# Strassen-like half products for the r and k tiles of the recurrence, their weight sums on GpSimd and their joins on VectorE

## The chip, the cores and the metric

One core of one Trainium2 chip runs the whole step. The metric is the device time of one execution in microseconds (us). All data are float32.

## The reference, cut to what matters

Two layers of a decoder trunk for 256 prompt positions and 8 single samples, 264 columns in all. Layer 0 is an attention layer with a paged cache, layer 1 an RWKV-7 layer. The changed work is the projection of layer 1 on its r, k and v columns:

```
h = rmsnorm(x, g_pre)                                    # 264 x 2048
p_shift, q_mem, gate = jnp.split(h @ w_in, RWKV_SPLITS, axis=-1)
prev = jnp.concatenate([shift_prev, p_shift[:, :-1]], axis=1)
s = p_shift + (prev - p_shift) * mu
r, k, v, wl, al = jnp.split(s, SHIFT_SPLITS, axis=-1)    # r, k, v: 1536 columns each
...
S = S * w_t + (S @ -kk_t) (kk_t * a_t) + v_t k_t         # per head of 64, over the positions
y_t = S @ r_t
return x + rmsnorm(out @ w_o, g_post)
```

The 24 heads are handled in 12 pairs of heads, 128 columns each of r, k and v.

## The kernel before

The program gives each engine its own list of instructions and orders them by semaphores written out by hand. `hT` holds the normed activations, 16 tiles (k) of 128 rows by T = 264 columns. The weights of a pair (`wrkv`, 128 x 16 x 384, 3 MB) lie in one of two slots `runit`; SyncE (SP) loads the next into the slot that has come free (L635 and L636).

**Turns.** The recurrence is a loop over turns o = -2 to 12 (`turn_of`, one for each engine: TensorE L1140, ScalarE L1636, VectorE L2256). In turn o the weights of pair o + 2 are multiplied ("fill"), pair o + 1 is prepared (token shift, decays, keys, four masked 128 x 512 matrices, the samples' state, the inverses of 16 x 16 blocks), pair o is solved and its outputs formed, and pair o - 1 gets its group norm. Turns 0 to 9 have all of these or all but the last. TensorE's turn is a list of small steps between which twelve calls of `project_part` (L1146) are laid; each does 4 of the 48 matmuls of a pair: parts 0 to 3 are the r tile, 4 to 7 the k tile, 8 to 11 the v tile. A tile accumulates in psum bank 0 or 1 in turn; `p_done` counts finished tiles, `p_free` tiles that were read (it starts at 2).

**ScalarE** copies each tile out in `projected(t)` (L1648): to `pb` (L1663), the last prompt and the sample columns to `shout` (L1664), and scaled by 1 - mu to `pm` (L1665). In the order of its turn: `projected(0)`, the turned rows, the solve's copies, `projected(1)`, more of these, `projected(2)`; then the masked pieces (L1759), two stores (L1763, L1766), and at the start of the next turn a table load and the sigmoids (L1718, L1719). VectorE's `mix` (L2277) waits for all three tiles.

**VectorE** in a turn: mix, keys, the 16-wide diagonal blocks (L2352), decays, normal keys, `scaled` (L2319 to L2322), `level(0)` (L2272), four matrices times masks (L2326), the state (L2401 to L2411), `blocks` (L2333), and the samples' outputs (L2414, L2415), whose end (`prepared`) TensorE's `lora` (L1165) of the next turn awaits. `blocks` is 28 dependent sums and products on 32 partitions (L2341, L2343) that wait for two small DMA steps of SyncE (`blocks` at L603: eight issues at L608, one at L610); in its middle VectorE gives TensorE the scaled state (L2331), for which `from_state` (L1276) waits, ahead of part 9. The solve's end is copied at L2420 to L2426.

**The same trick elsewhere.** The output projections already multiply a 2 x 2 block of weights by a 2 x 2 block of inputs with seven products of half size (`few_products`, L788): 8 matmuls of 132 columns each. There VectorE forms the weight sums (`weight_sums`, L2055 to L2060), the input sums (`input_sums`, L2039 to L2045) and joins the products (`joined`, L2068 to L2077). `w_sum`, `t_sum` and `y_out` count them.

**Around it.** `xT` holds the residual, which is not read between the start of the recurrence and the last residual sum. `qT1` (4 x 264 columns) holds the memory queries of layer 1; after turn -2 only its last 8 columns each are read. GpSimd (POOL) issues the transfers of the attention layer, idles in the recurrence, and issues the last cache loads (L703) when the last pair is solved. After the recurrence SP loads the units of gate and output weights (`late_unit`, L618, DMA at L621).

Of the kernel before, what the change touches and what calls it, by code (L numbers as in the profile page):

```python
# [13 lines left out]
P = 128  # L14
# [6 lines left out]
FH = 12  # L21
# [218 lines left out]
def trunk_step(nc, I, O):  # L240
    ctx = ExitStack()
    with ctx:
# [216 lines left out]

        def few_slot(i):  # L460

            layer, v = FEW[i]
            return (v - PLAIN0) % 3 if layer == 0 else (v + 8) % 3
# [59 lines left out]
        solvedT = nc.dram_tensor("solved_t", (4, 8, BLK * BLK), F32, kind="Internal").ap()  # L523

# [6 lines left out]
        def _(sp):  # L531
# [91 lines left out]
            for o in range(-1, RP - 1):  # L623
# [23 lines left out]
                blocks(o + 1)  # L647
            for v in range(3, 16):
# [47 lines left out]


# [12 lines left out]
        def _(pe):  # L710
# [77 lines left out]
            def few_products(i):  # L788
# [7 lines left out]
                if i >= 2:  # L796
                    pe.wait_ge(sem("y_out"), 2 * (i - 1))
# [12 lines left out]
                pe.wait_ge(sem("t_sum"), 4 * (layer + 1))  # L810
                product(Q4, a22, t4)
                pe.wait_ge(sem("w_sum"), 4 * i + 3)
# [3 lines left out]
                pe.wait_ge(sem("w_sum"), 4 * i + 4)  # L816
# [323 lines left out]
            def turn_of(o):  # L1140
# [5 lines left out]
                def project_part(n):  # L1146
# [6 lines left out]
                    if n == 0:  # L1153
                        pe.wait_ge(sem(f"r_full{b}"), 16 * ((o + 2) // 2 + 1))
                    if n % 4 == 0:
                        pe.wait_ge(sem("p_free"), m + 1)
                    if o == -2 and t == 0:
# [4 lines left out]
                    if n % 4 == 3:  # L1162
                        last.then_inc(sem("p_done"), 1)

# [219 lines left out]
        def _(act):  # L1384
# [15 lines left out]
            def output_tile(layer, j):  # L1400
# [10 lines left out]
                act.wait_ge(sem("y_out"), j - 2 * PLAIN0 + 1 if layer == 0 else 2 * FEW0 + j + 1)  # L1411
# [224 lines left out]
            def turn_of(o):  # L1636
# [11 lines left out]
                def projected(t):  # L1648
# [8 lines left out]
                    m = M_RKV + 3 * (o + 2) + t  # L1657
                    if t == 0:
# [6 lines left out]
                    ac(pm[:, t, :], psum[:, m % 2, 0:T], ACT.Copy, scale=om[:, b, t:t + 1]).then_inc(sem("p_free"), 1)  # L1665

# [127 lines left out]
        def _(dve):  # L1794
# [238 lines left out]
            def input_sums(layer, part):  # L2033
# [3 lines left out]
                done = lambda n: dve.wait_ge(sem("t_sum"), 4 * layer + n)  # L2037
# [9 lines left out]
            def weight_sums(i):  # L2047
# [9 lines left out]
                dve.wait_ge(sem("w_sum"), 4 * i + 1)  # L2057
                tt(s2, s1, a11, ALU.subtract).then_inc(sem("w_sum"), 1)
                dve.wait_ge(sem("w_sum"), 4 * i + 3)
# [196 lines left out]
            def turn_of(o):  # L2256
# [10 lines left out]

                def level(n):
# [129 lines left out]
                if prepare:  # L2398
# [4 lines left out]

# [44 lines left out]
            ch.do(v_.reciprocal(rs1, rs1))  # L2448
# [106 lines left out]
```

## Time and profile before

| | us |
|---|---|
| median of 3 runs (lowest, highest) | 1744.52 (1740.86, 1747.26) |
| the profiled execution: its time | 1743.76 |
| the profiled execution: span of the core | 1742.1 |
| TensorE / VectorE / ScalarE / GpSimd busy | 1622.8 / 1059.1 / 392.3 / 160.8 |
| turns of the recurrence, o = -2 to 12 | about 956 to 1528 |

The span is what the profile's times count from; the profiled execution's own time is 1.7 us longer. A matmul of float32 shows as two MATMUL records and two LDWEIGHTS records (PEld, the weight load beside it). Idle time in brackets is that of the engine just before the instruction, with what ended it. The turns of the recurrence repeat with the same rows; one of them, from TensorE's L1228 at 1250.22 us to its return at 1293.17, is read below.

### The profile page before, as it was taken

To read this page: it belongs to the slowest core of one execution; us is meant where nothing else is said; L and a number is where in the kernel's file an instruction comes from. 1 tells how busy PE (TensorE), PEld (TensorE's weight loads), DVE (VectorE), ACT (ScalarE), POOL (GpSimd) and SP (SyncE) were. 2 spreads that over 40 slices of the span, in tenths; PEclk is the share of its full clock that TensorE was granted. 3 is DMA by queue.
4 is the path that set the end of the run, shared out by engine and by line. 5 is a ranking of instruction groups with operands and counts; after the bars stand their busy time and mean duration, and the time that the engine had idled before them with its cause. 6 is when DMAs were issued, how large, how long until landed. Compare 5 with 4: busy or idle time off the path is not lost.

```text
span 1742.1 us, 27840 instructions
## 1 busy us (share of the span) xinstructions
PE 1622.8 (93%) x9596; PEld 1290.3 (74%) x9596; DVE 1059.1 (61%) x4997; ACT 392.3 (23%) x978; POOL 160.8 (9%) x295
## 2 busy tenths in 40 slices
PE   7979999899999999988989999999999999999995
PEld 6657776677677777657977777777777777788895
DVE  4587555655465555437872467777777777340755
ACT  2112011201121111221120433333333333221011
POOL 1012111221111211220000000000000000020000
PEclk9989999999999999999989999999999999999998
DMA  9579999999999999995442233333332323374441
GB/s 384 206 284 373 420 417 397 379 396 420 405 400 422 418 420 412 357 372 234 146 189 96 102 102 103 101 101 101 101 100 101 102 76 115 108 271 170 145 146 51
DMA packets 101725, 419.95 MB, mean 241 GB/s; under 512 B 41796, under 2 KB 46288, under 8 KB 91984
## 3 DMA queue, kind: packets, MB, share of 16 engines
q0 software_dynamic: 41680, 218.91, 31.6%
q1 hardware_dynamic: 53256, 187.54, 28.4%
q10 hardware_dynamic: 6648, 11.73, 1.8%
q8 instruction: 76, 1.25, 0.3%
q14 instruction: 65, 0.53, 0.1%
HBM read 405.28 MB, written 12.85 MB: 240 GB/s over the span
## 4 chain that ended last, share of the span: by engine, by line
PE 75%; DVE 10%; DMA 6%; ACT 5%; issue 2%; SPq 0%; POOLq 0%; POOL 0%; ACTq 0%; DVEq 0%
PE psum L733 25%; PE psum L801 10%; PE psum L1160 10%; PE psum L783 6%; PE psum L1023 5%; DMA kvr<-in_cv 3%; PE psum L722 2%; PE psum L771 2%; PE psum L1207 2%; DMA kvr<-in_ck 1%; PE psum L1217 1%; PE psum L744 1%; PE psum L759 1%; PE psum L824 1%; ACT gT L1759 1%
## 5 line engine op out<-in xcount | busy, mean ns | idle before, releaser
L1920 DVE CUSTOM_DVE_ANT_0 kvr<-kvr,arena 128x128 f32<-128x128 f32 x1488 | 323.7, 287 | 115.3 <-DMA kvr<-in_ck 115.2
L733 PE MATMUL psum<-hT,wring 128*128 128x264 f32 x1536 | 367.9, 397 | 0.0
L733 PEld LDWEIGHTS psum<-hT,wring 128*128 128x128 f32 x1536 | 294.5, 195 | 67.9 <-issue 19.8
L1160 PE MATMUL psum<-hT,kvr 128*128 128x264 f32 x1152 | 283.3, 392 | 1.8 <-DVE hT L2248 1.8
L1160 PEld LDWEIGHTS psum<-hT,kvr 128*128 128x128 f32 x1152 | 214.0, 192 | 41.9 <-issue 8.9
L1920 DVE DVE_READ_ACCUMULATOR2_ANT arena<- 128x1 f32 x1488 | 122.4, 82 | 0.0
L783 PE MATMUL psum<-hT,kvr 128*128 128x264 f32 x512 | 120.2, 391 | 0.0
L783 PEld LDWEIGHTS psum<-hT,kvr 128*128 128x128 f32 x512 | 96.9, 193 | 16.2 <-issue 0.4
L667 POOL DMA_DIRECT2D kvr<-in_cv x128 | 67.7, 529 | 371.7 <-PE psum L1023 275.0
L1023 PE MATMUL psum<-kvr,arena 128*32 128x384 f32 x1024 | 97.1, 495 | 4.9 <-DMA kvr<-in_cv 4.9
L667 POOL DMA_DIRECT2D kvr<-in_ck x128 | 67.6, 528 | 235.0 <-issue 228.0
L801 PE MATMUL psum<-hT,wring 128*128 128x132 f32 x672 | 77.9, 277 | 0.0
L801 PEld LDWEIGHTS psum<-hT,wring 128*128 128x128 f32 x672 | 76.7, 191 | 0.0
L703 POOL DMA_DIRECT2D wring<-in_cmk x8 | 5.8, 722 | 744.8 <-PE psum L1306 744.8
L1023 PEld LDWEIGHTS psum<-kvr,arena 128*32 128x32 f32 x1024 | 27.0, 109 | 49.8 <-issue 41.2
L733 PE MATMUL psum<-oT,wring 128*128 128x256 f32 x256 | 57.7, 382 | 0.0
L733 PE MATMUL psum<-gT,wring 128*128 128x256 f32 x256 | 57.4, 382 | 0.0
L801 PE MATMUL psum<-gT,kvr 128*128 128x132 f32 x448 | 53.0, 277 | 2.3 <-DVE gT L2030 2.3
L733 PEld LDWEIGHTS psum<-gT,wring 128*128 128x128 f32 x256 | 48.0, 190 | 9.1 <-issue 3.1
L733 PEld LDWEIGHTS psum<-oT,wring 128*128 128x128 f32 x256 | 47.9, 191 | 9.1 <-issue 2.5
L801 PEld LDWEIGHTS psum<-gT,kvr 128*128 128x128 f32 x448 | 51.6, 191 | 3.0 <-DVE gT L2030 1.6
L2326 DVE TENSOR_TENSOR wring<-psum,wring 128x512 f32<-128x512 f32 x48 | 30.9, 686 | 33.2 <-PE psum L1207 32.1
(433 smaller groups left out, 2315.2 us busy)
## 6 DMA issues: line engine op xcount, KB each, us to landing
kvr<-in_ck POOLq DMA_DIRECT2D x128, 768.0 KB, 11.8
kvr<-in_cv POOLq DMA_DIRECT2D x128, 768.0 KB, 11.5
kvr<-in_wrkv SPq DMA_DIRECT2D x12, 3072.0 KB, 13.8
kvr<-in_wo SPq DMA_DIRECT2D x14, 2048.0 KB, 8.1
wring<-in_wkv SPq DMA_DIRECT2D x12, 2048.0 KB, 11.8
wring<-in_wm SPq DMA_DIRECT2D x8, 2048.0 KB, 11.9
wring<-in_wg SPq DMA_DIRECT2D x8, 2048.0 KB, 12.1
kvr<-in_wg SPq DMA_DIRECT2D x8, 2048.0 KB, 9.1
```

The source lines that it names most:

```text
L667: pool.dma_start(ring[:, n % KRING, :], I["c" + name][bass.ds(pid, 1)].rearrange("a p n -> (a p) n"))\
L722: last = mm(psum[:, bank, 0:n], w[:, k, t * P:(t + 1) * P], rhs[:, k, 0:n], start=(k == 0), stop=(k == KT - 1))
L733: last = mm(psum[:, m % 2, 0:n], w[:, k, t * P:(t + 1) * P], rhs[:, k, 0:n], start=(k == 0), stop=(k == KT - 1))
L744: last = mm(psum[:, t, 0:T], w[:, k, t * P:(t + 1) * P], hT[:, k, :], start=(k == 0), stop=(k == KT - 1))
L771: last = mm(psum[:, m % 2, 0:T], w[:, k, t % 2 * P:(t % 2 + 1) * P], hT[:, k, :], start=(k == 0), stop=(k == KT - 1))
L783: last = mm(psum[:, m % 2, 0:T], w[:, k, t * P:(t + 1) * P], hT[:, k, :], start=(k == 0), stop=(k == KT - 1))
L801: last = mm(few_bank(i, q), w[:, k, :], x[:, k, :], start=(k == 0), stop=(k == KT // 2 - 1))
L1023: last = mm(Vp[32 * c:32 * c + 32, 0:384], Ps[:, n % 2, j * FH:j * FH + 32], ring[:, v % VRING, c * 384:(c + 1) * 384], start=(j == 0), st ...
L1160: last = mm(psum[:, m % 2, 0:T], w[:, k, t * P:(t + 1) * P], hT[:, k, :], start=(k == 0), stop=(k == KT - 1))
L1207: last = mm((A, B)[h][:, n * 256:(n + 1) * 256], src[hp, c * P:(c + 1) * P], KR[hp, a, c, :], start=True, stop=True)
L1920: last = v_.tensor_tensor_reduce(page, page, qb[:, n % 2, h * P:(h + 1) * P], 1.0, 0.0, ALU.mult, ALU.add, S[:, n % 2, j * FH + h:j * FH + ...
L2326: tt(GM[:, a, q, :], (A, B)[q % 2], masks[:, K_RM:K_RM + 512], ALU.mult).then_inc(sem("gm_out"), 1)
```

## The change

For pairs 1 to 11 of 0 to 11 (the second to the twelfth) the r and k tiles are taken together as a 2 x 2 block of weights (the halves of k by r and k columns; `pair_weights`), and multiplied by the 2 x 2 block of `hT` (the halves of k by 132 columns) with seven products of eight matmuls. The v tile stays as it was. The rows of the pair, 56 half products and 16 v matmuls (every second of 32 rows), are dealt out to the twelve parts by twelfths. The input sums stand in `xT`, whose contents go to DRAM and back; GpSimd makes them once. GpSimd also makes the four weight sums of each pair: one set of 1024 columns in the memory queries' place (`wsum1`), used twice, and two in place over the weights. Joins are nine operations of VectorE in three groups, and ScalarE copies r and k from `pb` and no longer from psum.

```diff
+        psums = xT[:, :, :].rearrange("p k t -> p (k t)").rearrange("p (s k t) -> p s k t", s=4, k=KT // 2)
+        wsum1 = qT1[:, :, 0:2 * P].rearrange("p h (j n) -> p h j n", j=2)
+        ROWS = [(q, k) for q in (Q2, Q1, Q5, Q4, Q7, Q6, Q3) for k in range(KT // 2)]
+        ROWS += [(Q3 + 1, k // 2) for k in range(2 * KT)]
+        CUT = [len(ROWS) * n // 12 for n in range(13)]
...
             for j in range(2):
                 pair(j, "wrkv", runit[:, j, :], f"r_full{j}")
                 pair(j, "vrkv", vunit[:, j, :], f"v1_full{j}")
+            sp.wait_ge(sem("x_new"), 4)
+            sp.dma_start(xkept, xT[:, :, :].rearrange("p k t -> p (k t)")).then_inc(sem("x_in2"), 16)
             sp.wait_ge(sem("p_done"), M_LORA + 2)
             unit(I["wqm1"], 1, 0)
...
                 blocks(o + 1)
+            sp.wait_ge(sem("p_done"), M_RKV + 3 * RP)
+            sp.dma_start(xT[:, :, :].rearrange("p k t -> p (k t)"), xkept).then_inc(sem("x_in2"), 16)
             for v in range(3, 16):
                 late_unit(v)
...
+            pt_ = nc.gpsimd.tensor_tensor
...
+            pool.wait_ge(sem("at_t"), 2 * MH + FH)
+            for u in range(1, RP):
+                m, at0 = M_RKV + 3 * u, 4 * (FEW0 + u - 1)
+                a11, a12, a21, a22 = pair_weights(u % 2)
+                pool.wait_ge(sem(f"r_full{u % 2}"), 16 * (u // 2 + 1))
+                if u > 1:
+                    pool.wait_ge(sem("w_sum"), at0)
+                    pool.wait_ge(sem("p_done"), m - 1)
+                pt_(wsum1, fold(a21), fold(a22), ALU.add).then_inc(sem("w_sum"), 1)
+                pool.wait_ge(sem("w_sum"), at0 + 1)
+                pt_(a21, a11, a21, ALU.subtract).then_inc(sem("w_sum"), 1)
+                pool.wait_ge(sem("p_done"), m + 1)
+                pt_(wsum1, wsum1, fold(a11), ALU.subtract).then_inc(sem("w_sum"), 1)
+                pool.wait_ge(sem("w_sum"), at0 + 3)
+                pt_(fold(a12), fold(a12), wsum1, ALU.subtract).then_inc(sem("w_sum"), 1)
...
+                def pair_part(n):
...
+                    for at in range(CUT[n], CUT[n + 1]):
+                        q, k = ROWS[at]
+                        if at in (0, 24, 48):
+                            pe.wait_ge(sem("p_free"), m + at // 24 + 1)
+                        if q > Q3:
+                            if at % 2 == 0:
+                                last = mm(psum[:, m % 2, TH:TH + T], w[:, k, 2 * P:3 * P], hT[:, k, :], start=(k == 0), stop=(k == KT - 1))
+                                if k == KT - 1:
+                                    last.then_inc(sem("p_done"), 1)
+                            continue
+                        if k == 0:
+                            if q == Q5:
+                                pe.wait_ge(sem("t_sum"), 8)
+                                pe.wait_ge(sem("w_sum"), sums + 1)
+                            if q == Q7:
+                                pe.wait_ge(sem("w_sum"), sums + 2)
+                            if q == Q6:
+                                pe.wait_ge(sem("w_sum"), sums + 3)
+                            if q == Q3:
+                                pe.wait_ge(sem("w_sum"), sums + 4)
+                        s = wsum1[:, k // 2, k % 2, :]
+                        lhs, rhs = {Q2: (a12, b21), Q1: (a11, b11), Q5: (s, t1), Q4: (a22, t4), Q7: (a21, t3), Q6: (s, t2),
+                                    Q3: (a12, b22)}[q]
+                        last = mm(pair_bank(o, q), s if q in (Q5, Q6) else lhs[:, k, :], rhs[:, k, :],
+                                  start=(k == 0), stop=(k == KT // 2 - 1))
+                        if at in (23, 47):
+                            last.then_inc(sem("p_done"), 1)
...
+                def pair_projected(t):
...
+                    if t == 0:
+                        return
+                    if t == 1:
...
+                        act.wait_ge(sem("y_out"), sums + 1)
+                        ac(pm[:, 1, :], pb[:, 1, 1:T + 1], ACT.Copy, scale=om[:, b, 1:2])
+                        ac(shout[:, 3 * (o + 2) + 1, :], pb[:, 1, NPR:T + 1], ACT.Copy)
+                        ac(pm[:, 0, 0:TH], pb[:, 0, 1:rest], ACT.Copy, scale=om[:, b, 0:1])
+                        return
+                    act.wait_ge(sem("p_done"), m + 3)
+                    act.wait_ge(sem("y_out"), sums + 2)
+                    v = psum[:, m % 2, TH:TH + T]
+                    ac(pb[:, 2, 1:T + 1], v, ACT.Copy)
+                    ac(shout[:, 3 * (o + 2) + 2, :], v[:, NPR - 1:T], ACT.Copy)
+                    ac(pm[:, 2, :], v, ACT.Copy, scale=om[:, b, 2:3])
+                    ac(pm[:, 0, TH:T], pb[:, 0, rest:T + 1], ACT.Copy, scale=om[:, b, 0:1])
+                    ac(shout[:, 3 * (o + 2), :], pb[:, 0, NPR:T + 1], ACT.Copy).then_inc(sem("p_free"), 1)
...
                 solution(0)
-                projected(1)
+                if not -2 < o < RP - 2:
+                    projected(1)
                 right_side(1)
                 right_turned(1)
                 solution(1)
+                if -2 < o < RP - 2:
+                    projected(1)
                 projected(2)
...
+                def joined_pair(part):
...
+                    dve.wait_ge(sem("p_done"), m + part + 1)
+                    if part == 0:
+                        ch.do(v_.tensor_copy(r1_, q(Q1)))
+                        v_.tensor_copy(k1_, q(Q5))
+                        tt(r0_, r1_, q(Q2), ALU.add).then_inc(sem("p_free"), 1)
+                    elif part == 1:
+                        ch.do(tt(r1_, r1_, q(Q6), ALU.add))
+                        ch.do(tt(k0_, r1_, q(Q7), ALU.add))
+                        ch.do(tt(r1_, r1_, k1_, ALU.add))
+                        ch.do(tt(k1_, k1_, k0_, ALU.add))
+                        ch.do(tt(k0_, k0_, q(Q4), ALU.add))
+                        dve.sem_inc(sem("p_free"), 1)
+                        dve.sem_inc(sem("y_out"), 1)
+                    else:
+                        tt(r1_, r1_, q(Q3), ALU.add).then_inc(sem("y_out"), 1)
...
                     ch.do(tt(s3, s3, bs(lw), ALU.mult))
-
+                    joined_pair(0)
                     dve.wait_ge(sem("z_y"), 2 * (o + 1) + 1)
...
                     blocks()
+                    joined_pair(1)
                     dve.wait_ge(sem("z_y"), 2 * (o + 1) + 2)
                     ch.do(tt(x3(Z[:, 1, :]), x3(B), i64, ALU.mult))
                     v_.tensor_reduce(ys[:, a, :], x3(Z[:, 1, :]), AX.X, ALU.add).then_inc(sem("prepared"), 1)
+                    joined_pair(2)
...
+            dve.wait_ge(sem("x_in2"), 48)
             for c in range(4):
                 residual(c, rs1).then_inc(sem("x_out"), 1)
```

`joined_pair` and `pair_projected` do their work in turns -1 to 9. Three products of a pair share a psum bank (`pair_bank`): Q2, Q1, Q5 in the first, Q4, Q7, Q6 in the second, Q3 and the v tile in the first again. The input sums of GpSimd are four 128 x 1056 operations behind a wait for the copy of `xT` out and for `hT`.

## Rows read from the trace of the kernel before

**Rows 1.** One turn by windows: PE, PEld, DVE, ACT, POOL busy; PEclk, DMA, GB/s.

```profile
1079.30:1121.92 42.62, 41.00 (x234) 32.05 (x234) 33.16 (x86) 15.06 (x42) 0.00 (x0) 1.00 0.32 103
```

**Rows 2.** Chain of waits, one turn: start, us, what.

```profile
1254.72 1.78 PE psum L1160 x8
...
1257.72 1.28 DVE wring L2326 x2
...
1269.81 0.36 DVE arena L2331
...
1276.85 0.05 ACT arena L1663
...
1281.59 0.37 DVE arena L2293
```

**Rows 3.** Chain of waits: half products of layer 0; turn -1.

```profile
879.93 17.56 PE psum L801 x156
...
1001.75 3.78 PE psum L1160 x8
```

**Rows 4.** VectorE's groups by form, 780 to 900 us: busy us, mean ns.

```profile
L2055 DVE TENSOR_TENSOR wring<-kvr 128x1024 f32<-128x1024 f32 x6 | 7.3, 1219 | 0.0
...
L2072 DVE TENSOR_TENSOR arena<-arena,psum 128x132 f32<-128x132 f32 x6 | 1.8, 294 | 8.3 <-PE psum L801 8.3
```

**Rows 5.** Timeline of VectorE and TensorE, one turn.

```profile
1261.22 0.69 DVE L2405 TENSOR_TENSOR gT<-psum,arena 128x512 f32<-128x512 f32 x1 [1.03 <-PE psum L1217]
...
1266.69 0.16 DVE L2341 TENSOR_TENSOR kmT<-kmT 32x14 f32<-32x14 f32 x1 [1.87 <-DMA kmT<-near]
...
1274.74 0.69 DVE L2415 TENSOR_REDUCE arena<-gT 128x8 f32<-128x512 f32 x1
...
1277.86 0.29 DVE L2420 COPY gT<-psum 128x128 f32<-128x128 f32 x1 [2.44 <-PE psum L1306]
...
1289.96 1.95 PE L1160 MATMUL psum<-hT,kvr 128*128 128x264 f32 x8
...
1290.56 0.43 DVE L2319 TENSOR_TENSOR wring<-arena 128x256 f32<-128x256 f32 x1 [0.26 <-ACT arena L1734]
```

**Rows 6.** Timeline of ScalarE, 1277 us.

```profile
1277.14 0.17 ACT L1664 ACTIVATE arena<-psum 128x9 f32<-128x9 f32 x1
1277.20 0.48 ACT L1665 ACTIVATE arena<-psum,arena 128x264 f32<-128x264 f32 x1
1277.56 0.51 ACT L1759 ACTIVATE gT<-wring 16x64 f32<-16x64 f32 x2
```

**Rows 7.** Timeline of TensorE, turns -1 and 0.

```profile
998.01 1.08 PE L1193 MATMUL psum<-cst,arena 128*128 128x128 f32 x6 [2.25 <-DVE arena L2322]
...
1024.14 0.68 PE L1171 MATMUL psum<-arena,kvr 96*128 96x264 f32 x2 [2.31 <-DVE arena L2415]
```

**Rows 8.** L1920 on VectorE: durations in ns, smallest, median, largest.

```profile
L1920 DVE CUSTOM_DVE_ANT_0 kvr<-kvr,arena x1488: 272/288/298, 62.9 to 711.4; 128x128 f32<-128x128 f32 x186
```

**Rows 9.** Windows of 910 to 925 us, columns as in rows 1.

```profile
910.00:915.00 5.00, 5.00 (x17) 3.40 (x16) 4.90 (x6) 3.54 (x9) 0.00 (x0) 0.68 1.00 423
...
920.00:925.00 5.00, 5.00 (x25) 3.64 (x24) 0.00 (x0) 0.00 (x0) 0.00 (x0) 1.00 0.01 2
```

**Rows 10.** Timeline of SyncE's issues, and of TensorE at 1528 us.

```profile
925.60 0.33 SPq L546 DMA_DIRECT2D wring<-in_wqm  x1
...
1491.06 62.25 SPq L621 DMA_DIRECT2D kvr<-in_wg  x4
...
1528.33 1.97 PE L783 MATMUL psum<-hT,kvr 128*128 128x264 f32 x4
```

**Rows 11.** DMA issues: count, KB each, us from issue to landing.

```profile
xT<-in_xT SPq DMA_DIRECT2D x1, 2112.0 KB, 8.0
```

**Rows 12.** TensorE by windows, turn -1: PE busy, PEclk, DMA, GB/s.

```profile
1000.00:1005.00 5.00, 5.00 (x16) 0.50 0.15 41
...
1025.00:1030.00 5.00, 5.00 (x27) 1.00 0.67 180
```

More of the change, by code:

```diff
@@ L694, in _ @@
                     page("v", *((kring, "k_full") if in_keys else (vring, "v_full")), n, STREAMS[i], n - KST[i])
+            pt_ = nc.gpsimd.tensor_tensor
+            pool.wait_ge(sem("x_in2"), 32)
+            pool.wait_ge(sem("h_out"), 16)
+            lo, hi = hT[:, 0:KT // 2, :], hT[:, KT // 2:KT, :]
+            b11, b12, b21, b22 = lo[:, :, 0:TH], lo[:, :, TH:T], hi[:, :, 0:TH], hi[:, :, TH:T]
+            t1, t2, t3, t4 = (psums[:, n, :, :] for n in range(4))
+            pt_(t1, b12, b11, ALU.subtract).then_inc(sem("t_sum"), 1)
+            pt_(t3, b22, b12, ALU.subtract).then_inc(sem("t_sum"), 1)
+            pool.wait_ge(sem("t_sum"), 4 + 1)
+            pt_(t2, b22, t1, ALU.subtract).then_inc(sem("t_sum"), 1)
+            pool.wait_ge(sem("t_sum"), 4 + 3)
+            pt_(t4, b21, t2, ALU.subtract).then_inc(sem("t_sum"), 1)
+            pool.wait_ge(sem("at_t"), 2 * MH + FH)
[13 more added lines that the diff above has]
+                pt_(fold(a12), fold(a12), wsum1, ALU.subtract).then_inc(sem("w_sum"), 1)
             pool.wait_ge(sem("y_y"), 2 * RP)
@@ L796, in few_products @@
                 if i >= 2:
-                    pe.wait_ge(sem("y_out"), 2 * (i - 1))
+                    pe.wait_ge(sem("y_out"), 2 * (i - 1) + 2 * UNITS1 * layer)
                 def product(q, w, x):
@@ L815, in few_products @@
                 product(Q7, s3, t3).then_inc(sem("few_y"), 1)
-                pe.wait_ge(sem("w_sum"), 4 * i + 4)
+                pe.wait_ge(sem("w_sum"), 4 * (i + UNITS1 * layer) + 4)
                 product(Q3, s4, b22).then_inc(sem("p_done"), 2)
@@ L1163, in project_part @@
                         last.then_inc(sem("p_done"), 1)
+                def pair_part(n):
+                    a11, a12, a21, a22 = pair_weights(b)
+                    t1, t2, t3, t4 = (psums[:, i, :, :] for i in range(4))
+                    b11, b21, b22 = hT[:, 0:KT // 2, 0:TH], hT[:, KT // 2:KT, 0:TH], hT[:, KT // 2:KT, TH:T]
+                    sums = 4 * (FEW0 + o + 1)
+                    m = M_RKV + 3 * (o + 2)
+                    for at in range(CUT[n], CUT[n + 1]):
[25 more added lines that the diff above has]
+                            last.then_inc(sem("p_done"), 1)
                 def lora():
@@ L2266, in turn_of @@
                 zt = x3(Z[:, 0, :])
+                def joined_pair(part):
+                    if not -2 < o < RP - 2:
+                        return
+                    m, lhs, rest = M_RKV + 3 * (o + 2), slice(1, 1 + TH), slice(1 + TH, 1 + T)
+                    r0_, r1_, k0_, k1_ = pb[:, 0, lhs], pb[:, 0, rest], pb[:, 1, lhs], pb[:, 1, rest]
+                    q = lambda n: pair_bank(o, n)
+                    dve.wait_ge(sem("p_done"), m + part + 1)
[13 more added lines that the diff above has]
+                        tt(r1_, r1_, q(Q3), ALU.add).then_inc(sem("y_out"), 1)
                 def level(n):
```

36 lines of the change are left out of this document (29 added, 7 removed).

## Prediction, made before the changed kernel ran

> **What bounds the kernel now.** The stage that changes, the recurrence, is a steady machine: nine of its turns take 42.6 to 43.0 us each, of which TensorE is busy 41.0 us, VectorE 33.2 and ScalarE 15.1, with a granted clock of 1.00; GpSimd does nothing there [rows 1]. TensorE busy for 41.0 of 42.6 us invites the reading that every matmul removed is time won. The chain of waits says otherwise [rows 2]. Read one turn from 1250.2 us on: TensorE holds the chain until 1257.7 us, then VectorE masks two matrices (L2326), SyncE issues eight small transfers, two transfers follow, VectorE solves blocks from 1266.7 us, and its L2331 at 1269.8 us releases TensorE's L1276. Only then does the chain run over projection parts 9, 10 and 11, to 1276.8 us. There it leaves TensorE again: ScalarE copies the v tile out (L1663 to L1665), copies six masked pieces, loads a table and computes the sigmoids for which VectorE's L2293 waits; the two hand on to each other until VectorE releases TensorE's L1228, where the next turn begins. So of twelve parts of the projection the chain holds four (4, 9, 10, 11); the others are filler beside VectorE, ScalarE and transfers.
>
> **What the half products give.** For pairs two to twelve, 32 matmuls of 264 columns become 56 of 132. A matmul is two records; the eight records of a part, four matmuls of 264, take 1.78 us in the chain, 0.445 us a matmul [rows 2]. 156 records of L801, the same half product elsewhere, take 17.56 us, 0.225 us a matmul [rows 3]. So 14.24 us become 12.60: 1.64 us less TensorE work a pair, 18 us over eleven. On the chain it is less. The 88 rows of the new list are dealt out by twelfths: part 4 holds seven half products (1.58 us for 1.78: 0.20 us less), parts 9 and 11 still four v matmuls, part 10 three (1.34 for 1.78: 0.44 less). That is all the chain can gain, 0.64 us a turn, and the 0.44 counts only if TensorE's last matmul still releases ScalarE.
>
> **The joins on VectorE.** Each is 128x132 with an input in PSUM: 0.29 us as at L2072 [rows 4], about 0.31 with the wait for its own semaphore. The first group (two copies, one sum, 0.9 us) stands between L2402 and L2405, where VectorE idles 1.03 us: nothing. Were that idle time gone, the 1.87 us before L2341, spent waiting for a transfer, would still cover it [rows 5]. The second group, five chained sums, 1.55 us, stands between the blocks and L2414; the third, one sum, 0.31 us, behind L2415. Before, VectorE finished L2415 at 1275.43 us and then idled 2.44 us [rows 5]; now the last join is through at 1275.43 - 0.20 + 1.55 + 0.31 = 1277.09 us. ScalarE began on the v tile at 1276.85 us and now waits for that join (the new wait on y_out; queued behind it are the masked pieces, the table and the sigmoids, and VectorE waits for those). That is 0.25 us later, and it takes the place of TensorE's gain. Behind the wait ScalarE has five operations for three: one more copy of 132 columns, one of nine. By the steps from start to start, 0.06 us after L1664 and 0.36 after L1665 [rows 6], half of the latter plus the former, 0.24 us, is the lower bound and 1.5 times the latter the upper, 0.54; I take 0.40, nearer the middle since a copy of half the columns costs over half. So the tail of a turn costs 0.65 us, ten times (turns 0 to 9): 6.5 us. In turn -1 TensorE waits for L2415 itself, 2.31 us already [rows 7], and the five sums less the 0.20 add 1.35 us. Together about 8 us. The r and k copies that leave the middle of ScalarE's turn save nothing: it idles there.
>
> **The weight sums on GpSimd.** Four a pair, 128x1024. No row has GpSimd arithmetic. The nearest is VectorE's own sum of that shape, 1.22 us (L2055) [rows 4]; I take d = 1.22 us as the lower end, twice that, 2.44, as the upper (an engine fetching its two inputs in turn), and the middle, 1.83. They are in time in any case: the third and fourth have from row 23 (part 3) to rows 40 and 48 (parts 5 and 6), over 10 us; the first two need the next unit, which lands 13.8 us after its issue, a turn ahead. Behind them GpSimd's queue has only cache loads after the last turn. The question is what they do to VectorE, which reads the same SBUF. GpSimd issuing transfers leaves VectorE's two-input L1920 alone, 272 to 298 ns over 1488 [rows 8]; nothing shows GpSimd reading operands. The price lies between nothing (independence) and one engine standing while the other runs. No row is nearer to either; I take the second at somewhat better than even, since both would read two full-rate operands from the same partitions, a load that no row shows borne without loss.
>
> Then place decides. The first two sums are released by row 47 in part 6, about 1265.2 us: they end at 1265.2 + d and 1265.2 + 2d. VectorE's blocks, 28 chained sums of 0.2 us with gaps into which GpSimd can slip, want to start at 1266.5 us and lose (1.83 - 1.3) + 1.83 = 2.4 us. The third sum is released by row 23, the second row of part 3, which began at 1289.96 us; that is some 0.1 us before VectorE's L2319 to L2322, four operations with both inputs in SBUF and on the chain, which stand idle 0.26 us before [rows 5]: 1.7 us. The fourth falls beside L2272 and the reciprocal, with one SBUF operand each. Sum: 3d - 1.4 = 4.1 us a turn, 45 us over eleven.
>
> The Trainium skill (SBUF — State Buffer, Who interferes with whom) has it that a VectorE instruction with two SBUF inputs and a GpSimd instruction that reads SBUF exclude each other for the whole instruction; no run shown here can confirm it. The same skill's GPSIMD Engine Reference (Elementwise — side-by-side cycle accounting) gives GpSimd's sum 1.96 times VectorE's; by it the collisions would be 5.8 us a turn and the time near 1816.
>
> **The residual and the queues.** The copy of xT out, 2112 KB, enters SP's queue about 911 us; the transfers of that moment run at 423 GB/s and are through before 920, when the DMA engines stand idle to 925 [rows 9]; the next issue, L546, comes at 925.60 [rows 10]. 2112 KB at that rate are 5.0 us: it fits. Without the gap the memory queries would wait those 5 us once. The copy back stands ahead of L621 at 1491.06 us; it and the unit's load, 8.0 us each as the residual's load before [rows 11], end before 1528.33, when TensorE first turns to that unit [rows 10]. The four input sums on GpSimd run beside turn -2 and are wanted some 20 us later. All nothing.
>
> **Sum.** 8 + 45 = 53 us on the profiled execution's 1743.76 us (span 1742.1; the median of the runs, 1744.52, is 0.8 us more): 1797 us. With d from 1.22 to 2.44 the collisions are 2.3 to 5.9 us a turn, and the time 1777 to 1817.
>
> **Rivals.** *A: no collision.* Only the joins and ScalarE's two operations are left: 1752 us; ScalarE's bounds make it 1750 to 1753, and a step of 0.08 us either way in each of the six joins on the path 1745 to 1758. For it: no row shows a conflict. Against: none of them could. *B: faster.* TensorE's own queue, not the chain, sets the turn, and the 1.64 us come off each: 1726 us. It decides at L1663, where ScalarE would have to go on earlier than 1276.85 us. For it: 41.0 of 42.6 us busy [rows 1]. Against: VectorE's idle 2.44 us were the only room in the tail, and 1.86 us of joins go into it. *C: collisions, and the clock.* TensorE would stand some 2.4 us before L1276 and 1.7 before L1193. In turn -1 it stood 2.25 us before L1193, the granted clock was then 0.50 for 5 us (1.2 for 2.4 GHz), and eight records took 3.78 us for 1.78; after the 2.31 us at 1024 the clock stayed at 1.00 [rows 3, 7, 12]. One such loss of 2.0 us a turn is 22 us more, 1819; two are 1841.
>
> **How the numbers follow.** Forecast 0.50, A 0.25, B 0.12, C 0.13. A measurement of this kernel tells about 0.5% (8.7 us) from no change. Faster: nearly all of B, 0.11. Within: A up to 1753, 0.15, and edges, 0.17. Slower: the rest, 0.72. The range leaves out B and the worst of C: 1746 to 1834.
>
> **What would show it.** Turns of 46 to 48 us for 42.6; L2319 to L2322 or the blocks' sums with durations or gaps of a microsecond and more where a GpSimd sum runs; ScalarE's copy of v released by the last join; TensorE waiting for L2331. Turns of 43.3 us with VectorE's durations unchanged would be A; under 42 us, B; v matmuls at half speed, C. GpSimd sums above 3 us, or TensorE waiting on w_sum, would break the sum in another place.

## The result: 1808.0 us, 3.7% slower, and the profile after

The changed kernel takes 1808.01 us, the median of 4 runs (1803.30 to 1809.51), against 1742.69 for the kernel before beside it: a ratio of 1.0374, 95% interval 1.0351 to 1.0396. The forecast was 1797 with a range of 1746 to 1834. The profiled execution took 1808.59 us, its span is 1806.9 and its mean granted clock 0.958 (0.980 before).

The page's first part, of the changed kernel: busy time, share of the span, instructions of each engine.

```profile
span 1806.9 us, 29104 instructions
PE 1644.6 (91%) x10124; PEld 1325.5 (73%) x10124; DVE 1150.5 (64%) x5096; ACT 389.7 (22%) x967; POOL 281.5 (16%) x343
```

For this stage the page misleads twice. TensorE, from which 18 us of work were taken, was busy 1622.8 us before and is now at 1644.6. VectorE, which got some 2.5 us of joins a pair (28 us over eleven), has risen by 91 us, from 1059.1. Both engines are busy with the same work for longer. The windows say where: turn -1, turn 1, a steady turn and the last with half products (columns as in rows 1).

```profile
989.04:1033.91 44.87, 33.43 (x179) 26.94 (x178) 34.00 (x77) 9.14 (x20) 10.11 (x4) 0.81 0.24 80
1080.92:1133.04 52.12, 43.03 (x284) 35.19 (x283) 44.11 (x94) 14.85 (x41) 10.26 (x4) 0.93 0.25 84
1237.47:1285.25 47.78, 43.02 (x283) 35.46 (x283) 41.39 (x95) 14.85 (x39) 10.07 (x4) 0.93 0.32 109
1467.55:1510.86 43.31, 41.11 (x284) 34.38 (x283) 37.22 (x94) 14.83 (x39) 4.72 (x2) 0.96 0.24 75
```

A steady turn takes 47.78 us (turns 2 to 8, seven of them, 47.77 to 47.80) where it took 42.62 [rows 1]. TensorE is busy 2.0 us longer than before although it has 1.64 us less to do: the granted clock is 0.93 for 1.00. The last turn has two GpSimd sums for four and 43.31 us; that alone points at the sums.

The chain of waits of the steady turn, of the changed kernel (start, us, what). Its lines for those of rows 2 and 5: L2514 is the third group norm's product, L2557 the last product over the samples' state (it stands right before the blocks), L2487 the blocks, L2477 was L2331, L1370 was L1276, L1237 the v tile's matmuls, L2412 the last join, L1783 and L1784 are ScalarE's copies behind it.

```profile
1245.01 1.73 DVE arena L2513
1246.77 2.27 DVE gT L2514
...
1259.52 2.73 DVE gT L2557
1262.24 2.25 DVE kmT L2487
...
1267.43 0.36 DVE arena L2477
1267.84 1.22 PE psum L1370 x2
1269.06 2.84 PE psum L1237 x8
...
1273.73 1.85 PE psum L1237 x8
1275.60 0.30 DVE arena L2412
...
1276.45 0.37 ACT arena L1783
1276.82 0.29 ACT arena L1784
```

The order is that of rows 2, but without SyncE and its transfers: VectorE, held up, reaches the blocks after their transfer has landed. The new link, join to ScalarE, is there; in this turn the last join itself idles 0.69 us until TensorE's v tile (L1237) is through, so the five joins before it are covered. Three VectorE instructions have grown: 2.27, 2.73 and 2.25 us, 7.25 together. The timeline of GpSimd and VectorE in the same turn shows beside what.

```profile
1243.93 2.37 POOL L750 TENSOR_TENSOR arena<-arena,kvr 128x1024 f32<-128x1024 f32 x1 [27.27 <-PE psum L1254]
1246.38 2.35 POOL L752 TENSOR_TENSOR kvr<-kvr,arena 128x1024 f32<-128x1024 f32 x1
1259.03 2.67 POOL L746 TENSOR_TENSOR arena<-kvr 128x1024 f32<-128x1024 f32 x1 [10.30 <-PE psum L1254]
1261.78 2.68 POOL L748 TENSOR_TENSOR kvr<-kvr 128x1024 f32<-128x1024 f32 x1
```

```profile
1243.47 0.42 DVE L2468 TENSOR_TENSOR arena<-arena,gT 128x256 f32<-128x256 f32 x1
1243.80 1.21 DVE L2418 TENSOR_TENSOR gT<-vmr,psum 128x1024 f32<-128x1024 f32 x1
1244.93 1.80 DVE L2513 RECIPROCAL arena<-arena 128x264 f32<-128x264 f32 x1
1246.77 2.25 DVE L2514 SCALAR_TENSOR_TENSOR gT<-gT,lnv,arena 128x264 f32<-128x264 f32 x1
...
1258.79 0.69 DVE L2555 TENSOR_TENSOR arena<-arena,gT 128x512 f32<-128x512 f32 x1
1259.52 2.73 DVE L2557 TENSOR_TENSOR gT<-arena 128x512 f32<-128x512 f32 x1
1262.17 2.31 DVE L2487 TENSOR_TENSOR kmT<-kmT 32x14 f32<-32x14 f32 x1
```

Read the ends. L746 ends at 1261.70; L2557, 0.69 us elsewhere, ends at 1262.25. L748 ends at 1264.46; L2487, 0.16 us for 32x14 elements, ends at 1264.48. A VectorE instruction that meets a GpSimd sum stands until the sum is over, whatever its own size, and a sum that comes while a VectorE instruction is under way stands too: L746 and L748 take 2.67 for 2.36 us. But L2418, with one of its inputs in psum, and the reciprocal, with one input, run beside L750 at 1.21 and 1.80 us, as ever.

TensorE behind this, of the changed kernel:

```profile
1263.33 1.94 PE L1237 MATMUL psum<-hT,kvr 128*128 128x264 f32 x8
1267.84 1.22 PE L1370 MATMUL psum<-wring,arena 128*128 128x256 f32 x2 [2.57 <-DVE arena L2477]
1268.85 3.04 PE L1237 MATMUL psum<-hT,kvr 128*128 128x264 f32 x8
```

It stands 2.57 us until L2477 is through, and the next eight records take 3.04 us where those before took 1.94: that is the granted clock, 0.50 (1.2 of 2.4 GHz) from 1267.84 to 1269.00 us, and 1.00 again from 1271.90 on.

### The profile page after: what moved, and what is told of

It reads as the page before. It is cut to its first block, busy times and chain, and to the rows that moved or that the text cites. A ratio compares the mean times of both kernels' runs of the same rounds, so it can differ in the third digit from the quotient of the medians.

```text
span 1806.9 us, 29104 instructions
## 1 busy us (share of the span) xinstructions
PE 1644.6 (91%) x10124; PEld 1325.5 (73%) x10124; DVE 1150.5 (64%) x5096; ACT 389.7 (22%) x967; POOL 281.5 (16%) x343
## 4 chain that ended last, share of the span: by engine, by line
PE 69%; DVE 18%; ACT 6%; DMA 5%; issue 2%; SPq 0%; POOLq 0%; ACTq 0%; POOL 0%; DVEq 0%
PE psum L789 25%; PE psum L857 10%; PE psum L839 6%; PE psum L1079 5%; PE psum L1237 3%; PE psum L778 2%; DVE kmT L2487 2%; PE psum L827 2%; DMA kvr<-in_cv 2%; PE psum L1254 1%; DMA kvr<-in_ck 1%; DVE gT L2557 1%; PE psum L1322 1%; PE psum L1301 1%; DVE gT L2514 1%
## 5 line engine op out<-in xcount | busy, mean ns | idle before, releaser
L789 PE MATMUL psum<-hT,wring 128*128 128x264 f32 x1536 | 362.5, 392 | 0.0
L789 PEld LDWEIGHTS psum<-hT,wring 128*128 128x128 f32 x1536 | 289.9, 192 | 66.6 <-issue 19.7
L839 PE MATMUL psum<-hT,kvr 128*128 128x264 f32 x512 | 121.7, 394 | 0.0
L839 PEld LDWEIGHTS psum<-hT,kvr 128*128 128x128 f32 x512 | 97.5, 194 | 16.9 <-issue 0.4
L1237 PE MATMUL psum<-hT,kvr 128*128 128x264 f32 x352 | 99.0, 428 | 0.0
L1237 PEld LDWEIGHTS psum<-hT,kvr 128*128 128x128 f32 x352 | 73.9, 217 | 20.0 <-issue 6.0
L857 PEld LDWEIGHTS psum<-hT,wring 128*128 128x128 f32 x672 | 76.7, 190 | 0.0
L1254 PE MATMUL psum<-hT,kvr 128*128 128x132 f32 x528 | 72.7, 287 | 0.0
L1254 PEld LDWEIGHTS psum<-hT,kvr 128*128 128x128 f32 x528 | 69.2, 200 | 1.4
L750 POOL TENSOR_TENSOR arena<-arena,kvr 128x1024 f32<-128x1024 f32 x11 | 26.2, 2380 | 279.6 <-PE psum L1254 279.6
L789 PEld LDWEIGHTS psum<-oT,wring 128*128 128x128 f32 x256 | 47.8, 190 | 10.4 <-issue 2.5
```

The source lines that it names most:

```text
L750: pt_(wsum1, wsum1, fold(a11), ALU.subtract).then_inc(sem("w_sum"), 1)
L789: last = mm(psum[:, m % 2, 0:n], w[:, k, t * P:(t + 1) * P], rhs[:, k, 0:n], start=(k == 0), stop=(k == KT - 1))
L839: last = mm(psum[:, m % 2, 0:T], w[:, k, t * P:(t + 1) * P], hT[:, k, :], start=(k == 0), stop=(k == KT - 1))
L857: last = mm(few_bank(i, q), w[:, k, :], x[:, k, :], start=(k == 0), stop=(k == KT // 2 - 1))
L1237: last = mm(psum[:, m % 2, TH:TH + T], w[:, k, 2 * P:3 * P], hT[:, k, :], start=(k == 0), stop=(k == KT - 1))
L1254: last = mm(pair_bank(o, q), s if q in (Q5, Q6) else lhs[:, k, :], rhs[:, k, :], start=(k == 0), stop=(k == KT // 2 - 1))
```

## The experiments

The time is told apart in steps, from the whole change down, then built up again in a better order. All times are medians of at least 4 runs; the kernel before took 1741.9 to 1743.0 us beside them.

**1. Without any GpSimd sum.**

```
-pt_(wsum1, fold(a21), fold(a22), ALU.add).then_inc(sem("w_sum"), 1)
+pool.sem_inc(sem("w_sum"), 1)
```

and so for all four weight sums and the four input sums.

> The changed kernel with the four input sums and the forty-four weight sums on GpSimd left out (GpSimd only counts its semaphores on; the half products are made with whatever stands in their place), all joins, waits and matmuls kept. Theory (a GpSimd instruction that reads SBUF and a VectorE instruction that needs two SBUF reads exclude each other for their whole length): VectorE's L2557, L2487 and L2514 go back to 0.69, 0.16 and 0.49 us, a turn takes 43.0 to 43.5 us instead of 47.8, turn -2 is 4 us shorter, and the time is 1748 to 1757 us. Rival (the loss is in the joins, ScalarE's tail and the new waits, and VectorE's long records are waits that would be there anyway): above 1780 us.

1757.63 us (1756.13 to 1758.89), ratio 1.0082 [1.0061, 1.0104]. The sums cost 50 us. The time is 0.6 us above the range of the theory, less than its runs scatter. What is left, 15 us over the kernel before, is twice the 8 of the prediction, and the turns differ among themselves: 42.76 us at a clock of 1.00, up to 45.05 at less. Windows of this kernel: three of 5 us in the longest turn, the shortest turn, and the longest.

```profile
1197.12:1202.12 5.00, 4.73 (x34) 4.34 (x34) 3.58 (x14) 4.10 (x13) 0.00 (x0) 1.00 0.40 106
1202.12:1207.12 5.00, 2.29 (x6) 1.36 (x7) 4.05 (x9) 2.42 (x4) 0.00 (x0) 0.79 0.93 347
1207.12:1212.12 5.00, 5.00 (x25) 4.90 (x25) 4.33 (x10) 3.27 (x7) 0.00 (x0) 0.53 0.88 335
1242.17:1284.93 42.76, 39.79 (x284) 32.77 (x283) 35.62 (x94) 14.58 (x39) 0.00 (x0) 1.00 0.31 103
1197.12:1242.17 45.05, 42.07 (x283) 35.35 (x283) 35.80 (x95) 15.21 (x40) 0.00 (x0) 0.92 0.29 98
```

Early in a turn TensorE has parts 0 and 1 beside a chain of small operations between VectorE and ScalarE. Seven half products last 1.74 us where eight records of 264 columns lasted 1.94, and TensorE is busy only 2.29 of 5 us. Where that is followed by a clock of 0.53, the turn is long.

**2 and 3. GpSimd writes only; GpSimd copies.** The weight sums become `nc.gpsimd.memset(wsum1, 0.0)` (and so on), or `nc.gpsimd.tensor_copy(wsum1, fold(a21))` and so on.

> The changed kernel without the input sums, and with each weight sum replaced by a GpSimd memset of the same place and shape (128 x 1024), behind the same waits: GpSimd writes SBUF but reads nothing. Theory (what collides is GpSimd's reading): VectorE's instructions keep their lengths and the time is that of the kernel without sums, 1748 to 1757 us. Rival (any GpSimd instruction with an SBUF operand holds VectorE up): VectorE has records of over 1.5 us beside every memset, and the time lies above 1765 us.

> The changed kernel without the input sums, and with each weight sum replaced by a GpSimd copy of the same output and of one of its inputs: GpSimd reads one operand instead of two. Theory: a reader of one operand excludes VectorE's two-input instructions just the same, for as long as the copy takes; with copies of 1 to 1.5 us the time is 1760 to 1780 us, and VectorE's first two-input instruction beside a copy is longer by up to the copy. Rival (only an engine reading two streams takes VectorE's share away): as without sums, 1748 to 1757 us.

1757.82 us (1753.94 to 1762.04) with the writes, the same as with nothing there; 1763.0 (1759.75 to 1771.07) with the copies. L2557 in one line each (the durations are smallest, median and largest, ns): the changed kernel, writes, copies.

```profile
L2557 DVE TENSOR_TENSOR gT<-arena x12: 691/2726/2740, 1022.8 to 1543.2; 128x512 f32<-128x512 f32 x12
```

```profile
L2557 DVE TENSOR_TENSOR gT<-arena x12: 691/693/694, 1010.2 to 1488.7; 128x512 f32<-128x512 f32 x12
```

```profile
L2557 DVE TENSOR_TENSOR gT<-arena x12: 691/1405/1406, 1010.5 to 1498.9; 128x512 f32<-128x512 f32 x12
```

It is GpSimd's reading that holds VectorE up, not its writing, and not its being at work. A copy, at 1.04 to 1.38 us, does it too, for as long as it lasts.

**4. The kernel before, with 44 idle sums.** GpSimd adds the same weights into an unused tile, released as in the change; nothing reads the results, and the next load of a unit waits for them.

```
+pt_(scratch4, a21, a22, ALU.add).then_inc(sem("aside"), 1)
```

> The kernel before, nothing of the change in it but forty-four GpSimd sums of two 128 x 1024 blocks of the pair's weights into a place that nobody reads, released by the tiles nearest to where the change releases them (the k tile of the pair before, the r tile of the pair). All outputs are as before. Theory: the collisions alone are the larger part of the loss; GpSimd's sums take 2.4 to 2.7 us, a turn takes 46 to 48 us, and the time is 1782 to 1805 us. Rival (the loss needs the joins and half products, because TensorE's cover has become thinner): below 1755 us.

1801.49 us (1798.21 to 1808.74), ratio 1.0351 [1.0318, 1.0383]. Without half products, joins, new waits of TensorE on the sums or a moved residual, 59 us are lost. In this kernel the sums held VectorE in other places (in a turn 2.21 us in the group norm's product for 0.49, and 2.25 and 2.39 us in two of the blocks' sums for 0.19 and 0.20), and a turn took 47.8 us as well. Nothing of the loss needs the change's own structure.

**5. The changed kernel without the input sums.**

> The changed kernel with GpSimd's four sums over the inputs left out (their results are wrong, the semaphores are kept); the 44 weight sums stay. Theory (collisions, turn by turn): the turn before the first pair shrinks from 34.1 us to the kernel before's 30.1, the rest stays: 1804 us. Rival (the input sums cost nothing, as the prediction had it): 1808 us and that turn at 34.1.

1800.69 us (1796.74 to 1804.70), 7.3 us less by the medians, with some 4 us of scatter on either. The trace shows the 4.0 us that the theory named: from its first half part to the next turn's start, turn -2 takes 30.10 us for 34.11 (957.68 to 987.78; 954.93 to 989.04). The turns from -1 to 9 take 522.4 us for 521.8, so the rest of the 7.3 is not the recurrence's. The timelines of VectorE and TensorE in turn -2 of the changed kernel show how: two 128x256 TENSOR_SCALAR, 0.62 us without sums, meet input sums.

```profile
960.24 3.19 DVE L1949 TENSOR_SCALAR gT<-gT,arena 128x256 f32<-128x256 f32 x2
...
963.48 0.80 PE L892 MATMUL psum<-cst,gT 128*128 128x128 f32 x4 [2.11 <-DVE gT L1949]
```

**6. The sums where VectorE reads psum or waits.** Nothing left out; GpSimd gets further waits, as

```
+pool.wait_ge(sem("tl_in"), u)
 pt_(wsum1, wsum1, fold(a11), ALU.subtract).then_inc(sem("w_sum"), 1)
```

> The changed kernel with nothing left out; GpSimd additionally waits, so that its sums run beside VectorE work that does not read two inputs from SBUF: input sums each behind a head of the memory's weights, sum 1 behind the first joins of r and k of the pair before, sum 2 behind the cumulated decays (beside the reciprocal), sum 3 behind the four scaled tiles, sum 4 behind the first masked product. Theory (the loss of the sums is exclusion with VectorE's instructions of two SBUF inputs, a matter of the moment): turns of 43 to 45 us as without sums, 1757 to 1766 us. Rival 1 (GpSimd's sums slow VectorE or TensorE whatever runs beside them): above 1785. Rival 2 (TensorE now waits for sums that come too late): turns above 46 with idle time of TensorE ahead of half products released by GpSimd.

1763.68 us (1760.17 to 1765.58), ratio 1.0116 [1.0090, 1.0143]. The same 48 sums on the same engine, 44 us less. One was still ill placed (timelines of GpSimd and VectorE of this kernel, lines 9 lower than in the changed one):

```profile
1296.86 2.35 POOL L755 TENSOR_TENSOR kvr<-kvr 128x1024 f32<-128x1024 f32 x1 [9.42 <-DVE arena L2461]
```

```profile
1296.97 2.40 DVE L2465 TENSOR_SCALAR arena<-arena 128x264 f32<-128x264 f32 x1
1299.40 1.80 DVE L2466 RECIPROCAL arena<-arena 128x264 f32<-128x264 f32 x1
```

The wait for sum 2 was meant for the reciprocal, 0.4 us later. The TENSOR_SCALAR ahead of it has one input, and stands for the whole sum all the same, 2.40 for 0.29 us.

**7. No sums, and another deal of the rows.** To the first experiment:

```
-CUT = [len(ROWS) * n // 12 for n in range(13)]
+CUT = [0, 7, 21, 28, 34, 41, 48, 54, 62, 68, 74, 82, 88]
```

> The changed kernel without any GpSimd sum (semaphores only; wrong results, as in the first experiment, which took 1757.6), and with the 88 rows dealt otherwise over the 12 parts: the second part, which covers TensorE's waits for the key sums early in a turn, holds 14 rows for 7, the later ones 6 or 7 for 7 or 8. Theory (part of the 15 us that are left without the sums is TensorE's clock, which falls after waits that the thinner half products no longer cover): the mean granted clock rises from 0.968 towards 0.99, turns fall from 43.9 to about 42.7, 1742 to 1748 us. Rival (the joins and ScalarE's two further copies on the path at a turn's end make up those 15 us): no change, 1755 to 1760.

1748.87 us (1743.99 to 1752.31), ratio 1.0033 [1.0017, 1.0050]: 8.8 us less than with the even deal, for the same instructions. Turns are 42.3 to 42.4 us, some 43.3 to 43.6. The mean clock of the whole execution went from 0.968 to 0.977, not to the 0.99 expected (the kernel before has 0.98). In the turns themselves the theory holds: with the even deal the granted clock was 1.00 in two of the turns 1 to 9 and 0.92 to 0.96 in seven, with this deal 1.00 in all nine. The four turns of 43.3 to 43.6 us are long for another reason: in them VectorE waits 1.7 to 2.0 us ahead of the blocks for SyncE's small transfers, in the five others 0.7 to 0.8.

**8. Placed sums and that deal.**

> Both together, nothing left out: the sums placed as in the second kernel, the rows dealt as in the third. Theory: 1742 to 1752 us, so level with the kernel before. Rival (the first half product that needs a sum now comes right after the turn's start and waits for GpSimd's first sum, and the clock falls again): 1760 to 1775.

1774.71 us (1772.38 to 1778.63), ratio 1.0176 [1.0153, 1.0199]: the rival's figure, but not by the rival's way. Sum 2 again stretched the TENSOR_SCALAR (L2465, median 2398 ns), and with fewer half products beside it TensorE stood longer behind it, 2.5 us in nearly every turn, for 0.5 to 2.4 with the even deal. Its timeline in this kernel, where the eight L1331 take 1.16 us at the full clock:

```profile
1269.49 1.14 PE L1296 MATMUL psum<-cst,arena 128*128 128x128 f32 x6 [2.49 <-DVE arena L2477]
1270.62 2.08 PE L1331 MATMUL psum<-gT 128*128 128x128 f32 x8
```

**9 and 10. The placement mended, with the even deal and with the other.** Sum 2 now waits for the four scaled tiles, sum 3 for the first masked product, sum 4 for the second level's difference; for the second of the two also

```
+CUT = [0, 7, 21, 26, 32, 40, 48, 54, 62, 68, 74, 82, 88]
```

> The placed sums moved once more, nothing left out. In the trace of the first placement (1763.7 us) sum 2 stretched the scaled keys' lower bound, a TENSOR_SCALAR of one SBUF input, from 0.29 to 2.40 us on the chain. Now sum 2 waits for the four scaled tiles, sum 3 for the first masked product, sum 4 for the second level's difference; sum 1 stays behind the first joins. Theory: turns of 45.2 us lose about 1.5 to 2.1 us, 1744 to 1757 us, at or below the 1757.6 without sums. Rival (TensorE's waits at the turn's end set the turn, the stretched instruction was covered): 1760 to 1765.

> As the second placement, with the rows dealt so that the second part holds 14 of the 88 rows and the two parts behind it 5 and 6. Theory (thin cover early in the turn costs clock and time, as 1748.9 against 1757.6 us without sums showed): 1744 to 1752 us, 5 to 10 us under its sibling with the even deal. Rival (the first placement's 1774.7 with this deal against 1763.7 without it: fewer half products around the four scaled tiles let the clock fall there, whatever the sums do): 1765 to 1775.

1751.39 us (1746.75 to 1762.18), ratio 1.0074 [1.0044, 1.0105], and 1747.16 (1744.91 to 1754.13), ratio 1.0030 [1.0012, 1.0048]. The TENSOR_SCALAR is back at 0.29 us. Of the sums' 50 us nothing measurable is left; the 6 us by which the first lies under the kernel without sums is within the scatter of its five runs, and the deal's gain is smaller than without sums (the intervals touch).

**11. The second group of joins ahead of the blocks.**

```
-blocks()
 joined_pair(1)
+blocks()
```

> As the kernel with placed sums and the other deal, and the five joins of the second group ahead of the blocks' small inverses instead of behind them, where VectorE waits 0.76 us for the diagonal blocks' transfer anyway; sum 1 waits for the end of the blocks. Theory (the joins behind the blocks lie on the chain that ends a turn): 0.5 to 0.8 us less a turn, 1736 to 1744 us. Rival (the blocks start 0.85 us later, the state's scaling with them, and TensorE waits for it): no gain, or up to 6 us more.

1745.64 us (1743.09 to 1747.27), ratio 1.0019 [1.0008, 1.0030]. The gain, 1.5 us, is under what was expected and within the scatter of the runs: the profile gives 42.56 us a turn at a clock of 1.00, and shows TensorE waiting 0.76 us for the state's scaling, which stands inside the blocks and now comes later. So part of the rival holds. The best form of the change, then, is level with the kernel before (0.1 to 0.3% over it) and not faster. A window of one of its turns:

```profile
1192.31:1234.88 42.57, 39.77 (x285) 32.78 (x283) 35.55 (x94) 14.74 (x41) 9.44 (x4) 1.00 0.31 103
```

GpSimd is as busy as in the changed kernel (9.44 for 10.07 us a turn), and VectorE at 35.55 for 41.39: the 5.8 us between are standing, not work.

**12. Neither sums nor joins.** To the first experiment; the nine joins are left out, their semaphores kept, the even deal.

> The changed kernel without any GpSimd sum (as the first experiment, 1757.6 us) and also without VectorE's nine joins of r and k (their semaphores are kept, r and k keep old values); the half products, the even deal of the rows and ScalarE's eight copies stay. What is left against the kernel before is the half products with ScalarE's two further copies. Theory (the prediction's sum: the joins cost 8 us, the half products save 7): 1749 to 1751 us here is a confirmed join price, but the half products then save nothing and cost 7 to 8 us through their thin cover. Rival 1 (the joins are all of what is left): 1740 to 1744. Rival 2 (the joins lie beside TensorE's work and cost nothing): 1755 to 1759.

1740.91 us (1737.99 to 1742.33, 12 runs), ratio 0.9985 [0.9975, 0.9995]: rival 1. A turn of this kernel at the full clock:

```profile
1234.23:1276.17 41.94, 39.53 (x285) 32.70 (x283) 33.13 (x85) 14.73 (x40) 0.00 (x0) 1.00 0.31 105
```

## Why the prediction was right, and where it was off

By medians the change now comes apart so: kernel before 1742.7; half products and ScalarE's two copies -2 (1740.9); joins +17 (1757.6); weight sums where the change lets them run +43 (1800.7); input sums +7 (1808.0), of which the trace shows 4. In the profiled executions the turns -1 to 9 took 461.7, 460.4, 473.6, 522.4 and 521.8 us in this order, so joins 13 and weight sums 49. The shares also depend on the order of leaving out: put on the kernel before, the weight sums cost 59.

**The half products: too small on the chain.** The step said that of 1.64 us of TensorE's work only 0.64 a turn come off; less ScalarE's two further copies, priced at 0.40, that is 0.24 without sums and joins. At the full clock a turn went from 42.62 to 41.94 us, 0.68. The chains of a turn of 42.63 us of the kernel before, and of the turn of 41.94 us:

```profile
1121.92 1.16 PE psum L1228 x8
...
1134.01 1.98 PE psum L1160 x8
...
1146.36 1.85 PE psum L1160 x8
...
1148.69 0.37 ACT arena L1665
1149.06 0.12 ACT gT L1759
```

```profile
1250.09 1.16 PE psum L1322 x8
...
1273.48 1.85 PE psum L1237 x8
...
1275.93 0.37 ACT arena L1783
1276.30 0.29 ACT arena L1784
...
1276.69 0.12 ACT gT L1882
```

From the turn's L1228 (L1322) to the end of the last v matmul TensorE takes 25.24 us for 26.29, so the half products give 1.05 us, not 0.64. From ScalarE's scaled copy of v to its masked pieces it is 0.76 us for 0.37: the two copies cost 0.39, as priced (0.40). The step that was off is the reading of the chain. Of the turns 1 to 9 of the kernel before, the one of rows 2 is the only one whose chain runs through SyncE and its transfers; it took 42.96 us. In the other eight TensorE holds the chain from its L1228 through parts 4 to 11, eight parts and not four.

Over eleven turns 0.68 would be 7 us, and 2 were measured (1740.91 to the 1743.04 beside it): other turns of that kernel took 42.3 to 43.7 us. In five of its turns 1 to 9 VectorE waits 1.7 to 2.4 us ahead of the blocks for SyncE's small transfers (42.4 to 43.7 us a turn), in the four others 0.5 to 1.1 (41.9 to 42.3); in those five, and only there, the chain runs through these transfers. The same waits of 1.83 and 1.87 us in two turns of the kernel before lengthened these by only 0.3 to 0.4 us. Only two of the five long turns have a lower clock (0.96). So the thinner cover gave the rest back in two ways, to transfers that it no longer hides and to the clock, and the first took at least as much; why the transfers take longer in some turns, no run here shows.

**The joins: right at the full clock, the total not.** The step let the joins swallow TensorE's 0.64 us and add 0.25, together 0.89 a turn; at the full clock a turn went from 41.94 to 42.76 (42.51 in the kernel of experiment 2), 0.6 to 0.8 us, and in that turn ScalarE does wait for the last join. Half products, joins and ScalarE's copies together were priced at 0.65 us a turn and are only 0.1 at the full clock (42.76 to 42.63), since the half products gave more. Yet they cost 15.5 us in all and not 8. What was left out is what waits do beyond their length. In experiment 1 the granted clock was under 1.00 in seven of the turns 1 to 9, and in four VectorE waited 1.9 to 2.3 us for the small transfers; dealt otherwise, the same instructions took 8.8 us less, with the clock at 1.00 in all nine. Rival C had TensorE's clock after a wait, but only behind collisions.

**The collisions: mechanism right, two places wrong, and the size a little low.** 45 us were priced, 43 measured for the weight sums (49 by the traces of the recurrence). The parts differ more. d was 2.36 us, and 2.67 where a VectorE instruction was already under way, not 1.83; the upper bound, 2.44, would have been nearly right. The first two sums met VectorE where the step said, at the end of part 6, but one instruction earlier: L2557 stood 2.03 us extra, L2487 2.15; less the idle time before the blocks that this used up. The third was released right behind the four scaled tiles in place of 0.1 us before them: those ran undisturbed. TensorE's clock had moved it: in the steady turn L1322, ahead of row 23, took 1.92 us at the half clock, in turn 1, at the full clock, 1.05. The fourth, free by the step, outlasted the reciprocal and stretched L2514 by 1.76. What a microsecond decides shows in turn 1 of the changed kernel, where the third sum came 0.1 us after the first scaled tile and not 1.5:

```profile
1094.79 2.57 DVE L2466 TENSOR_TENSOR wring<-arena,gT 128x256 f32<-128x256 f32 x1
1097.28 2.56 DVE L2467 TENSOR_TENSOR arena<-arena,gT 128x256 f32<-128x256 f32 x1
```

Two instructions of 0.42 us, and a turn of 52.12. The steady turns grew by 47.78 - 42.62 = 5.2 us, of which half products, copies and joins are 0.1 at the full clock; the rest, 5.1, stands against the 4.1 of the sum, and some 1.6 of it is TensorE's clock behind L1370, which the sum left to rival C. That 45 and 43 lie so close is in part luck: with the measured 2.36 in the step's own places the sum is 3 x 2.36 - 1.4 = 5.7 us a turn, 62 over eleven; the third sum mostly missed, the fourth hit unforeseen, and the kernel without the sums was already 7 us slower than the step had it.

**The rule of the Trainium skill.** The page SBUF — State Buffer, Who interferes with whom, which no run could confirm before, fits: a VectorE instruction with two SBUF inputs and a GpSimd instruction that reads SBUF exclude each other for the whole instruction (0.69 us became 2.73), and one that only writes does not. The estimate of 1816 us, worked out with the ratio of the GPSIMD Engine Reference, was nearer to 1808 than the forecast, by the same luck of places; the ratio was 2.36 to 1.22, 1.93 for its 1.96. The sentence that the prediction took from the page is not its whole rule: the same section also lists copy and tensor_scalar, in the modes that use both ports, as instructions that can contend. The TENSOR_SCALAR with one SBUF input that was held 2.40 us agrees with that; it takes 0.29 us for 128x264 from SBUF and 0.43 from psum.

**The input sums: wrong.** Costed at nothing as work wanted only later. Late they were not; but they too read SBUF while VectorE does. The step looked at their due time and not at what they run beside, the very question it put to the weight sums. The copies of xT out and back cannot be told from nothing: experiment 12 keeps them and is 0.15% under the kernel before.

**The rivals.** A, no collision, falls with experiment 4 and with L2557's durations. B, faster, falls with experiment 12: without sums and joins 0.15% is all there is. Its mechanism is partly there, TensorE's queue on the chain for most of a turn, but 1.05 of the 1.64 us come off, and ScalarE takes 0.39 back. C is half true: one wait a turn before L1370 costs some 1.6 us of clock (3.04 for 1.94, 1.22 for 0.70), and the wait of 1.23 us early in a steady turn is followed by half the clock too (L1322 1.92 for 1.05), but other waits went unpunished, and the total stayed below 1819.

## What to carry to other kernels

An idle engine is not free room: GpSimd's sums cost 50 us or nothing measurable, for the same sums, by what VectorE does at that moment. Before giving GpSimd arithmetic, list the stretches in which VectorE reads psum, takes a reciprocal or waits, for at least the sum's own length, and gate each sum to start there. And price a removed matmul by the chain, read in several turns and not in one, then look at what it covered: shorter filler can cost more, in clock and in transfers that show, than it saves in work.

## What the runs showed of the hardware that was not expected

- A VectorE TENSOR_SCALAR from SBUF to SBUF with a single input (128x264, 0.29 us) stood 2.40 us for a GpSimd sum; a RECIPROCAL of the same shape (L2513, 1.80 us) ran beside a sum undisturbed. No run here varies the property that tells them apart; the rows show that the TENSOR_SCALAR takes less from SBUF than from psum (0.29 us, 0.43 for 128x264).
- The held instruction's size does not matter: 32x14 elements stood 2.31 us.
- GpSimd pays too where VectorE was first: its sum took 2.67 us for 2.36, its copy 1.37 for 1.04; where the sum was first it kept its 2.36. Its 128x1024 memset took 0.95 in every place.
- Early in a turn of the first experiment TensorE stood 0.47, 0.68 and 1.23 us and the clock stayed at 1.00; in another turn it stood 1.06, 0.68 and 1.23 and the clock went to 0.53. What exactly tips it is left open.
